# A hybrid decoder step on one core: the delta-rule levels placed around half projection tiles

## The reference, cut to what matters

```python
kk = jnp.einsum('bhtd,bhsd->bhts', kc, kc)
mat = eye + jnp.where(strict, bc[..., :, None] * dec * kk, 0.0)
rhs = bc[..., None] * (vc - jnp.exp(b)[..., None] * jnp.einsum('bhtd,bhdv->bhtv', kc, S))
u = lax.linalg.triangular_solve(mat, rhs, left_side=True, lower=True, unit_diagonal=True)
qk = jnp.einsum('bhtd,bhsd->bhts', qc, kc)
o = jnp.exp(b)[..., None] * jnp.einsum('bhtd,bhdv->bhtv', qc, S) + jnp.einsum('bhts,bhsv->bhtv', dec * qk, u)
S = jnp.exp(b_last)[..., None] * S + jnp.einsum('bhsd,bhsv->bhdv', kc * jnp.exp(b_last - b)[..., None], u)
```

## Time and profile before

| | us |
|---|---|
| median of 3 runs | 2033.61 |
| lowest and highest | 2029.54 and 2034.94 |
| the profiled execution | 2029.31 |
| its span, first to last instruction | 2027.5 |

### The profile page before, as it was taken

The page is one execution under the profiler, slowest core; times in us unless marked ns, Lnnn a source line. Parts: engine busy times, 40 slices in busy tenths (PEclk is TensorE's granted clock), DMA queues, the critical chain, the costliest instruction groups (busy, mean ns, idle before and its releaser), DMA issues.

```text
span 2027.5 us, 28786 instructions
## 1 busy us (share of the span) xinstructions
PE 1917.1 (95%) x12304; PEld 1339.9 (66%) x12304; DVE 507.6 (25%) x1051; ACT 373.0 (18%) x766; POOL 121.7 (6%) x206
## 2 busy tenths in 40 slices
PE   8988899999899999999988999998969999999998
PEld 5777778787568888878877887866733343333334
DVE  3422253343531000043333424273230000000000
ACT  2232133433101000013121433320010010100001
POOL 2000000302200000000000002041000000000000
PEclk9999999999999999999998999999979999999999
DMA  9998668999979978567433768573447999869993
GB/s 304 350 365 299 224 244 307 359 314 339 398 248 385 364 283 321 205 229 263 146 135 130 248 215 287 177 262 136 153 158 262 371 374 407 330 221 385 372 408 131
DMA packets 254053, 563.10 MB, mean 278 GB/s; under 512 B 11629, under 2 KB 149073, under 8 KB 253648
## 3 DMA queue, kind: packets, MB, share of 16 engines
q1 hardware_dynamic: 235232, 500.14, 68.5%
q0 software_dynamic: 17904, 57.79, 8.5%
q10 hardware_dynamic: 784, 3.25, 0.4%
HBM read 547.35 MB, written 196.24 MB: 367 GB/s over the span
## 4 chain that ended last, share of the span: by engine, by line
PE 90%; DMA 3%; DVE 2%; ACT 2%; issue 2%; SPq 1%; DVEq 0%; POOL 0%; ACTq 0%; POOLq 0%
PE PS L774 36%; PE PS L1383 14%; PE PS L1409 7%; PE PS L879 4%; PE PS L1247 4%; PE PS L1287 4%; PE PS L767 3%; PE PS L1261 3%; PE PS L1345 2%; PE PS L872 2%; PE PS L1431 1%; DMA ring<-in_w_in 1%; PE PS L782 1%; PE PS L1184 1%; SPq L736 1%
## 5 line engine op out<-in xcount | busy, mean ns | idle before, releaser
L774 PE MATMUL PS<-h,ring 128*128 128x264 f32 x3328 | 770.8, 389 | 7.4 <-DMA ring<-in_w_in 5.8
L774 PEld LDWEIGHTS PS<-h,ring 128*128 128x128 f32 x3328 | 627.0, 191 | 132.8 <-issue 23.3
L1542 ACT COPY z<-PS 128x264 f32<-128x264 f32 (+3 forms) x307 | 130.8, 444 | 941.6 <-PE PS L774 599.3
L1383 PE MATMUL PS<-ring,z 128*32 128x512 f32 (+1 forms) x1440 | 212.2, 527 | 1.4 <-ACT z L1542 1.4
L1383 PE MATMUL PS<-arena,z 128*32 128x512 f32 (+1 forms) x1056 | 190.2, 535 | 0.0
L1383 PEld LDWEIGHTS PS<-ring,z 128*32 128x32 f32 x1440 | 67.8, 111 | 128.3 <-issue 112.7
L1409 PE MATMUL PS<-arena,z 128*32 128x512 f32 x432 | 104.0, 593 | 0.0
L1383 PEld LDWEIGHTS PS<-arena,z 128*32 128x32 f32 x1056 | 54.8, 110 | 54.0 <-issue 54.0
L1247 PE MATMUL PS<-z,ring 128*128 128x264 f32 x384 | 87.3, 388 | 0.0
L1383 PE MATMUL PS<-z 128*32 128x512 f32 x576 | 84.7, 593 | 0.0
L1409 PE MATMUL PS<-ring,z 128*32 128x512 f32 x480 | 83.5, 592 | 0.0
(11 more groups left out here) (313 smaller groups left out, 1736.7 us busy)
## 6 DMA issues: line engine op xcount, KB each, us to landing
out_win_s<-in_cache_win_kv SPq DMA_DIRECT2D x128, 1023.5 KB, 10.5
ring<-in_w_in SPq DMA_DIRECT2D x88, 1024.0 KB, 5.5
out_win_s<-in_cache_win_kv SPq DMA_DIRECT2D x32, 1022.0 KB, 10.0
ring<-in_moe_w_gate SPq DMA_DIRECT2D x28, 1024.0 KB, 9.6
arena<-in_moe_w_up SPq DMA_DIRECT2D x22, 1024.0 KB, 11.5
ring<-in_moe_w_up SPq DMA_DIRECT2D x22, 1024.0 KB, 8.3
ring<-in_moe_w_down SPq DMA_DIRECT2D x20, 1024.0 KB, 11.0
arena<-in_moe_w_down SPq DMA_DIRECT2D x18, 1024.0 KB, 10.4
```

The costliest lines, as they stand in the source:

```text
L774: last = mm(bank(*job)[:, 0:T], w(k), h[:, k, :], start=(k == 0), stop=(k == KT - 1))
L1383: last = mm(m_bank("c", "gu", g, b, w, r)[BLK * j:BLK * j + BLK, 0:n], hs[:, k, P * r + BLK * j:P * r + BLK * j + BLK], v3(slot_ap(set_slo ...
L1542: return nc.scalar.copy(out, in_)
```

## The change

A new helper `around` puts each GDN step's first half, four of the eight contraction steps of a projection tile (`proj_half`), the GDN step's second half, and the other four contraction steps, in this order. The steps are cut where TensorE needs another engine's answer: kk and qk before "at", the squares before xx0 and xx1, y before lx0 and lx1, u before oc and ds. The number of projection tiles in a pass stays nine. The turns and the right-hand side leave `gdn_st`: vt (TensorE) and its copy (ScalarE) go to level 0, ks and the scaling of R (VectorE) to level 1, kt, the exponential of dl and the scaling to kd to level 2. The mask products that make `t1` go one step earlier each: that of level 0 into the last square, that of level v + 1 to just behind y of level v.

```diff
@@ -83,13 +83,17 @@
+    def around(*step):
+        j = next(proj)
+        return [step, ("proj_half", j), (step[0] + "2", *step[1:]), ("proj", j)]
+
     for i in range(TT):
-        s += [("gdn_dec", i)] + p() + [("gdn_a", i)] + p()
+        s += [("gdn_dec", i)] + p() + around("gdn_a", i)
         for q in range(3):
-            s += [("gdn_sq", i, q)] + p()
+            s += around("gdn_sq", i, q)
         for v in range(3):
-            s += [("gdn_lv", i, v)] + p()
-        s += [("gdn_st", i)] + p()
+            s += around("gdn_lv", i, v)
+        s += around("gdn_st", i)
...
@@ -836,13 +849,25 @@
+            def proj_ks(l, j, ks):
+                n = CH0[l] + j // 2
+                if j % 2 == 0 and ks[0] == 0:
+                    wait_chunk(pe, n)
+                if ks[0] == 0:
+                    open_bank(pe, l, "p", j)
+                w = v3(chunk(n), KT)
+                for k in ks:
+                    last = mm(bank(l, "p", j)[:, 0:T], w[:, k, P * (j % 2):P * (j % 2) + P], h[:, k, :],
+                              start=(k == 0), stop=(k == KT - 1))
+                if ks[-1] == KT - 1:
+                    last.then_inc(full(l, "p", j), 1)
+
+            def proj_half(l, j):
+                proj_ks(l, j, range(4))
+                halved.add((l, j))
...
@@ -913,28 +942,35 @@
                 heads((l, "y", i, v), lambda n: t1[:, n, :], lambda n: X[:, n, :])
+                tok_ = slice(P * i, P * i + P)
+                if v == 0:
+                    turned(l, i, "vt", 8)
+                elif v == 2:
+                    turned(l, i, "kt", 4)
+                elif i:
+                    wait_read(pe, l, "ds", i - 1)
+                    heads((l, "ks", i), lambda q: c[:, 4 + q, tok_], lambda q: S[:, q, :])
+
+            def gdn_lv2(l, i, v):
                 wait_read(pe, l, "y", i, v)
                 wait_read(pe, l, *(("xx1", i, 2) if v == 0 else ("lx1", i, v - 1)))
...
@@ -2044,8 +2084,31 @@
+            def level(l, v):
+
+                tt(t1, AT, bc(K(("m32t", "m64t", "m128t")[v]), 1, [P, 4, P]), MUL).then_inc(sems["ot_ready"], 1)
+
             def gdn_lv(l, i, v):
-                tt(t1, AT, bc(K(("m32t", "m64t", "m128t")[v]), 1, [P, 4, P]), MUL).then_inc(sems["ot_ready"], 1)
+                wait_full(dve, l, "y", i, v)
+                if v < 2:
+                    level(l, v + 1)
+                if v == 1:
+                    wait_read(dve, l, "vt", i)
...
```

More of the change, by code:

```diff
@@ L137, in mixer_jobs @@
     if k == "gdn_a":
-        return [("kk", *a), ("qk", *a), ("at", *a)]
+        return [("kk", *a), ("qk", *a)]
+    if k == "gdn_a2":
+        return [("at", *a)]
     if k == "gdn_sq":
-        return [("sq0", *a)] + [("sq1", *a)] * (a[1] < 2) + [("xx0", *a), ("xx1", *a)]
+        return [("sq0", *a)] + [("sq1", *a)] * (a[1] < 2)
+    if k == "gdn_sq2":
+        return [("xx0", *a), ("xx1", *a)]
     if k == "gdn_lv":
-        return [("y", *a)] + [("lx0", *a)] * (a[1] < 2) + [("lx1", *a)]
+        return [("y", *a)] + [[("vt", a[0])], [("ks", a[0])] * (a[0] > 0), [("kt", a[0])]][a[1]]
+    if k == "gdn_lv2":
+        return [("lx0", *a)] * (a[1] < 2) + [("lx1", *a)]
     if k == "gdn_st":
-        return [("vt", *a)] + [("ks", *a)] * (a[0] > 0) + [("u", *a), ("oc", *a), ("kt", *a), ("ds", *a)]
+        return [("u", *a)]
+    if k == "gdn_st2":
+        return [("oc", *a), ("ds", *a)]
     if k == "gs_a":
@@ L763, in _ @@
             mm, tr = nc.tensor.matmul, nc.tensor.transpose
+            halved = set()
             def turn_over(out, in_, rows, **kw):
@@ L837, in small_turn @@
                 last.then_inc(full(l, "cba"), 1)
-            def proj(l, j):
[L840 to L845, removed]
+            def proj_ks(l, j, ks):
[13 more added lines that the diff above has]
+                halved.add((l, j))
+            def proj(l, j):
+                proj_ks(l, j, range(4, KT) if (l, j) in halved else range(KT))
             def conv_s(l):
@@ L920, in gdn_lv, with turned @@
                 heads((l, "lx1", i, v), lambda n: Y[:, n, :], lambda n: XT[:, n, :])
-            def gdn_st(l, i):
[L923 to L934, removed]
+            def turned(l, i, name, base):
+                open_bank(pe, l, name, i)
+                for q in range(CH):
+                    last = turn_over(bank(l, name, i)[:, P * q:P * q + P], c[:, base + q, P * i:P * i + P], P)
+                last.then_inc(full(l, name, i), 1)
+            def gdn_st(l, i):
                 pe.wait_ge(sems["r_ready"], V("r_ready", l, i))
@@ L1655, in gdn_lv @@
                 copy(Y, v3(bank(l, "y", i, v), 4)).then_inc(free(l, "y", i, v), 1)
+                if v == 0:
+                    wait_full(act, l, "vt", i)
+                    copy(R, v3(bank(l, "vt", i), 4)).then_inc(free(l, "vt", i), 1)
+                elif v == 2:
+                    act.wait_ge(sems["dlx_ready"], V("dlx_ready", l, i))
+                    act_(dl, dl, ACT.Exp).then_inc(sems["dl_ready"], 1)
             def gdn_st(l, i):
[L1658 to L1659 removed]
                 wait_full(act, l, "u", i)
                 copy(U, v3(bank(l, "u", i), 4)).then_inc(free(l, "u", i), 1)
[L1662 to L1663 removed]
                 wait_full(act, l, "oc", i)
@@ L2038, in gdn_sq @@
                     cp(PT, v3(bank(l, "sq1", i, q), 4)).then_inc(free(l, "sq1", i, q), 1)
+                else:
+                    level(l, 0)
                 wait_full(dve, l, "xx0", i, q)
@@ L2055, in gdn_lv @@
                 tt(XT, XT, v3(bank(l, "lx1", i, v), 4), SUB).then_inc(free(l, "lx1", i, v), 1)
-            def gdn_st(l, i):
[L2058 to L2077, removed]
+                if v == 2:
+                    dve.wait_ge(sems["dl_ready"], V("dl_ready", l, i))
+                    wait_full(dve, l, "kt", i)
+                    for q in range(CH):
+                        last = ts(kd[:, q, :], bank(l, "kt", i)[:, P * q:P * q + P], dl[:, q:q + 1], None, MUL)
+                    last.then_inc(free(l, "kt", i), 1)
+            def gdn_st(l, i):
                 wait_full(dve, l, "ds", i)
```

24 lines of the change are left out of this document (21 added, 3 removed).

## The result

The changed kernel takes 1986.34 us (median of 4 runs, 1977.88 to 1988.05) against 2034.28 before (4 runs, 2029.54 to 2035.07): ratio 0.9766, 95% interval 0.974 to 0.9792. The profiled execution, the shortest of the four, took 1977.88 us with a span of 1976.0, where the sum had left 1978.

What follows compares the result with a forecast made beforehand. GDN passes bound by TensorE's waits on other engines: 35.9 + 10.8 for restarts + 8.0 for the clock - 2.9 = 51.8 us, taken as 51.5; 2029.31 becomes 1978 profiled, median 2033.6 becomes 1982, range 1974 to 1992 (chance 0.80).

Steps and rivals of the forecast that it cites:

- What bounds the kernel: Four GDN passes, 280.4 us or 14% of the span: chains between engines, not full engines; TensorE's standing still matters.
- The waits and their restarts, 35.9 + 10.8 us: GDN passes: 40 TensorE waits for ScalarE and VectorE, 35.9 us, plus 0.27 each for the pipeline emptying and filling, 10.8.
- the 2.9 that come back: Ahead of the first square: a new wait of 0.63 us plus restart of about 0.10, four times, 2.9 us lost again.
- The clock, 8.0 us: Three GDN passes at granted clock 0.98, 0.95 and 0.93 lose 8.0 us in all, after standstills that the change removes.
- Half tiles inside cost nothing in themselves: Inside GDN steps: moving a 1.78 us half adds no matmul or gap; waits for Y, squares and U go.
- Cover behind the step: Behind each step: VectorE's answers have 1.78 us less cover; X for the next y keeps a margin of 0.6 to 0.7.
- The moves: R, kd, vt, ks, kt moved up: no instruction added, waits for R and kd go, with the standstills before clock drops.
- The turn: At "at": the wait of 0.53 us goes; one of 0.63 comes ahead of the first square, restart about 0.10.
- Transfers: Rival: layer 0 is bound by DMA transfers, so its half of the gain is lost; 2008 us, chance 0.07.
- Late answers: Rival: VectorE returns X, XT and R 1.4 us later, costing 12 us at 12 places; 1994 us, chance 0.07.
- No effect: Rival: TensorE would be late for weights or banks at each half anyway; 2034 us, chance 0.02.
- a falling clock: Rival: more bank and product changes bring the lower clock; one whole pass at 0.50 gives 2038 us, chance 0.04.

Runs made afterwards that it cites:

- six-inside kernel: Changed kernel with six of the eight contraction steps inside each GDN step and two behind it, in place of four and four: 1988.65 us, ratio 0.9794.
- the two partial kernels: Kernel before with one part of the change each: half tiles alone, 2008.07 us (0.9865); turns, R, kd and mask products moved alone, 2000.93 us (0.9835).
- halves-only kernel: Kernel before with half tiles inside each step; turns, R, kd and mask products stay where they were: 2008.07 us, ratio 0.9865.
- three and four copies: Changed kernel with three or four cache copies instead of two behind each of ten layer 0 weight loads: 1985.17 us (0.9776) and 2001.78 us (one run).
- moves only: Kernel before with turns, R, kd and mask products moved up, every projection tile whole behind its step: 2000.93 us, ratio 0.9835.

## Why the prediction was right

**What bounds the kernel.** Right: 99% of what the span lost lies in the four passes; outside them the differences of up to 2.1 us cancel to 0.4.

**The waits and their restarts, 35.9 + 10.8 us.** Shown by the sum: with the clock's 8.0 and the 2.9 that come back, the passes should lose 51.2 to 51.8 and lost 51.1; by groups 56.4 and 58.2 were forecast, 56.36 and 58.30 measured. The third pass shows it without the clock, which was 1.00 there before and after: forecast 66.98 - 56.4 = 10.6, measured 66.98 - 56.35 = 10.63. The 0.27 us for a restart holds where TensorE runs fully empty (0.73 shown, 1.00 lost). The six-inside kernel shows that a gap of 0.2 us costs 0.07 more, not 0.27.

**The clock, 8.0 us.** Right in size: set against the same rows at full clock, the slow rows of the three passes took 1.3, 2.8 and 3.9 us longer. Of the cause that I named, the waits for R and kd, the two partial kernels bear out the first part: falls only where both waits remain, but each begins behind R, and the wait for u, which the prediction named beside it, is gone in the halves-only kernel, which falls all the same. That the length of a wait decides is argued from eight waits for R, not shown by an experiment that changes it alone. And as the kernel before has one profile, how much of the 8.0 us another execution of it would lose is not known.

**Half tiles inside cost nothing in themselves.** Right; 32 tiles are cut and the passes are as long as their groups to 0.2 us. **Cover behind the step.** Right: the margin of 0.6 to 0.7 us that I gave it is 0.89 less in the six-inside kernel, which is short by 0.2. **The moves.** Right in sum; what I had passed over is that the mask products had to move with the halves: 6.7 us hang on it, though before they cost nothing.

**The turn.** The step was right, its size 0.06 large: the squares start 0.57 us late where 0.63 was worked out, and 0.10 for the restart comes on top of either.

**The rivals.** Transfers: excluded by the passes at three and four copies. Late answers: their mechanism exists (six inside), but begins only where the cover is 0.7 us shorter than in the changed kernel. No effect, and a falling clock: excluded by the clock of 1.00 in every pass of every kernel that has the moves. With it falls the outcome that the Trainium skill's rule ("TensorE: Matmul & The Clock Gate", section "A second HAM failure mode: psum-queue depth-cycling") would give here; the trace disagrees as far as the changes of bank go, since TensorE changes them more often than before and stays at 1.00. The page speaks of idle moments between the groups, in a kernel with bf16 products 512 wide; this change takes most of those moments away, and the kernel that keeps fifteen of them (moves only, all in float32) stays at 1.00 as well.

**The number.** That the 1978 left for the profiled execution met its 1977.88 is luck in part: two more profiled executions of the same kernel, with the same passes, took 1984.24 and 1986.00. 1982 was made for a median, and the three medians are 1986.3, 1984.2 and 1982.8. Against their medians of before (2034.3, 2033.8, 2032.5) the gains are 47.9, 49.5 and 49.7, where the passes give 51.1. The gains of the other versions miss what their passes give by as much and more, on both sides: from 6.3 us too little (three copies) to 4.7 too much (moves only). In the profiles such differences lie behind the last pass, where the clock falls differently. Whether the last 1 to 3 us are only this spread was not settled: the kernel before has one profile, and its stretch behind the passes could not be compared over many.

## What to carry to other kernels

A wait that took 0.7 us in the profile cost 1.0 here, where the engine ran empty, and filler work of one wait's length, cut from a product that is there anyway, removes both. Look for products that sum up over many steps: here cutting them behind two, four or six of eight steps cost nothing in itself. Count the cover on both sides of the cut: what leaves the gap behind a step lays bare whatever was hidden there (here a mask product, and the transpose's answer), so move that work first, and place each cut by the two margins, not in the middle. Before pricing a gap by its share of the span, look at the clock in the instructions behind it.

## What the runs showed of the hardware that I had not expected

Fifteen waits of up to 0.8 us in 126 us left the granted clock at 1.00 (moves only), while the passes with a standstill of 1.8 or 2.2 us and one of 1.3 had it between 0.93 and 1.00. In all five passes that fell, the lower clock began behind the wait for R: after each of four waits of 2.23 us, after one of four of 1.76, and behind none of the 1.3 us for kd. The same pass of the kernel before fell in layer 0 (0.98) and did not in layer 1 (1.00), with the same waits. Behind the passes the clock's falls differ from one execution to the next, and with them the stretch from 923.4 to 934.7 us: with one profile of most kernels, parts of a program must be compared and not its whole.
